# Taking the small loads' wait at the first chunk instead of the third, in a two-layer encoder kernel

## The reference

```python
def reference(x, norm_mix, norm_ffn, norm_final, ...):
    for i in range(DEPTH):
        h = rmsnorm(x, norm_mix[i])
        if i % N_MIXERS == 0:
            x = x + stick_breaking_mixer(h, sb_w_in[j], sb_w_out[j])
        else:
            x = x + mlstm_mixer(h, ml_w_in[j], ml_b_i[j], ml_b_f[j], ml_g_head[j], ml_w_out[j])
        h = rmsnorm(x, norm_ffn[i])
        x = x + hierarchical_moe(h, moe_w_group[i], moe_b_group[i], moe_w_expert[i], moe_b_expert[i],
                                 moe_w1[i], moe_w3[i], moe_w2[i])
    return rmsnorm(x, norm_final)
```

## Time and profile before

| | |
|---|---|
| median of 3 runs | 1768.82 us (1767.27 to 1771.22) |
| the profiled execution's own time | 1768.82 us |
| its span | 1767.1 us |
| TensorE busy (matmuls) | 1568.3 us, 89% |
| VectorE busy | 729.4 us, 41% |
| ScalarE busy | 423.4 us, 24% |
| GpSimd busy | 64.9 us, 4% |
| mean granted TensorE clock | 0.946 of full speed |

### The profile page before, as it was taken

One profiled execution on the slowest core, in us unless ns is written; L12 is line 12 of the kernel. 1 busy time (PEld: TensorE's weight loads), 2 busy tenths in 40 slices (PEclk: granted clock), 3 DMA queues, 4 the chain that ended last, 5 costly groups with the idle time before them and its releaser, 6 DMA issues.

```text
span 1767.1 us, 25607 instructions
## 1 busy us (share of the span) xinstructions
PE 1568.3 (89%) x9901; PEld 1074.5 (61%) x9901; DVE 729.4 (41%) x1167; ACT 423.4 (24%) x571; POOL 64.9 (4%) x90
## 2 busy tenths in 40 slices
PE   7999999999997788878799999999999887788775
PEld 7999999888543234423287988988864443243322
DVE  4454454443332222223264757657434232223223
ACT  5343443433000000000054334343320000000002
POOL 2210100100100000000011000000000000000000
PEclk9999999999998898889899999999999888998897
DMA  7645555578999999999954455566699999999996
GB/s 262 196 150 167 160 172 168 214 263 305 371 384 425 427 425 425 425 427 424 417 181 146 144 190 178 178 234 213 225 356 394 422 424 425 427 424 424 425 426 264
DMA packets 149643, 543.79 MB, mean 308 GB/s; under 512 B 8864, under 2 KB 25680, under 8 KB 116432
## 3 DMA queue, kind: packets, MB, share of 16 engines
q1 hardware_dynamic: 148448, 541.14, 78.8%
q0 software_dynamic: 1136, 1.82, 0.4%
HBM read 540.83 MB, written 2.10 MB: 307 GB/s over the span
## 4 chain that ended last, share of the span: by engine, by line
PE 58%; DMA 27%; issue 5%; SPq 5%; DVE 2%; ACT 2%; POOL 1%; POOLq 0%; DVEq 0%; ACTq 0%
PE psum_G L706 30%; DMA ring<-in_moe_w 26%; PE psum_S L706 16%; PE psum_A L706 7%; SPq L521 5%; PE psum_T L706 4%; DVE w_lo L421 1%; ACT w_hi L417 1%; ACT h L1365 0%; POOL arena L668 0%; ACT arena L1199 0%; PE psum_A L713 0%; DVE x L1710 0%; POOLq L642 0%; DVE h L1960 0%
## 5 line engine op out<-in xcount | busy, mean ns | idle before, releaser
L706 PE MATMUL psum_A<-ring,arena 128*32 128x512 f32 x2048 | 297.5, 711 | 146.3 <-DMA ring<-in_moe_w 142.5
L421 DVE TENSOR_TENSOR w_lo<-ring,w_hi 128x2048 fp32r<-128x2048 f32 x126 | 289.1, 2298 | 288.3 <-ACT w_hi L417 282.9
L417 ACT CAST w_hi<-ring 128x2048 fp32r<-128x2048 f32 x128 | 244.1, 1908 | 242.5 <-PE psum_G L706 154.3
L706 PEld LDWEIGHTS psum_A<-ring,arena 128*32 128x32 f32 x2048 | 68.5, 120 | 316.9 <-issue 315.1
L1843 DVE COPY arena_two<-psum_A 128x512 f32<-128x512 f32 x64 | 44.3, 692 | 382.6 <-PE psum_T L706 350.0
L1875 DVE TENSOR_TENSOR x<-x,psum_S 128x512 f32<-128x512 f32 x128 | 88.0, 688 | 168.7 <-PE psum_S L706 168.7
L706 PE MATMUL psum_G<-xT_hi,w_hi 128*128 128x256 f32 x512 | 148.7, 290 | 1.0 <-DVE w_lo L421 1.0
L706 PE MATMUL psum_G<-xT_hi,w_lo 128*128 128x256 f32 x512 | 144.8, 283 | 0.0
L706 PE MATMUL psum_G<-xT_lo,w_hi 128*128 128x256 f32 x512 | 144.7, 283 | 0.0
L706 PE MATMUL psum_G<-ring,arena_two 128*32 128x512 f32 x976 | 121.5, 618 | 16.1 <-DMA ring<-in_moe_w 16.0
L1381 ACT ACTIVATE arena_two<-psum_T 128x64 f32<-128x64 f32 x64 | 14.4, 224 | 488.6 <-PE psum_T L706 488.6
(11 more groups left out here) (239 smaller groups left out, 2124.0 us busy)
## 6 DMA issues: line engine op xcount, KB each, us to landing
ring<-in_moe_w SPq DMA_DIRECT2D x378, 1024.0 KB, 18.8
ring<-in_sb_w_in SPq DMA_DIRECT2D x48, 1024.0 KB, 5.0
ring<-in_ml_w_in SPq DMA_DIRECT2D x48, 1024.0 KB, 5.2
ring<-in_sb_w_out SPq DMA_DIRECT2D x16, 1024.0 KB, 4.9
ring<-in_ml_w_out SPq DMA_DIRECT2D x16, 1024.0 KB, 5.1
turned_slots<-in_moe_w SPq DMA_DIRECT2D x6, 1024.0 KB, 12.6
x<-in_x SPq DMA_DIRECT2D x2, 1024.0 KB, 6.0
out_x<-h SPq DMA_DIRECT2D x4, 512.0 KB, 2.8
```

The source lines that it names most:

```text
L417: act.copy(w_hi[:, slot_place(j), :], ring[:, slot_place(j), :]).then_inc(hi_made, 1)
L421: dve.tensor_tensor(w_lo[:, slot_place(j), :], ring[:, slot_place(j), :], w_hi[:, slot_place(j), :].bitcast(F32), ALU.subtract).then_inc(l ...
L706: return pe.matmul(dst, lhsT, rhs, start=start, stop=stop, skip_group_check=True)
```

## The change

The work that waits for the small loads is taken at the end of the first chunk of group 0 instead of at the end of the third: `split_gates` on ScalarE, `scale_router` on VectorE (in both layers), and `thresholds` and `gate_lo` on VectorE. No operation is added or removed, and no load is issued at another place.

```diff
@@ ScalarE, sb_group
                     if step == "chunk" and kind == "out" and k < XC - 1:
                         chunk_squares(0, k)
-                    if step == "chunk" and kind == "first" and k == 2:
+                    if step == "chunk" and kind == "first" and k == 0:
                         split_gates(act)
@@ VectorE, common_step (both layers)
                         take_chunk(layer, i, k)
-                    if kind == "first" and k == 2:
+                    if kind == "first" and k == 0:
                         scale_router(layer)
```

## The result

The changed kernel takes 1790.98 us (median of 4 runs, 1789.12 to 1791.99) against 1769.34 us for the kernel before on the same chip: 21.6 us slower, ratio 1.0121 with a 95% interval of 1.0104 to 1.0139. The forecast was 1790.2. The profiled execution took 1790.06 us; its span is 1788.3 us, against 1767.1.

What follows compares the result with a forecast made beforehand. TensorE was taken to bound the projection, the weight stream the experts. A hole of 21.3 us, plus 1.7 of clock, less 1.6 of old hole, gave +21.4 on 1768.8: 1790.2 us, range 1786 to 1798.

Steps and rivals of the forecast that it cites:

- The place of the hole: Group 0 of layer 0: TensorE, done with slot 6 at 58.0, waits for slot 7 until 79.3, 21.3 us.
- The pace of the small loads: GpSimd's eight `gate_w` loads: one at a time, 2.66 us for each interval once slot loads stop.
- The rival that kept the 5.5 us: Small loads keep their pace, 20th lands at 90.50 as before: +37 us, 1806; chance 0.06.
- the rival with 0.75 us: Small loads limited by issue time alone, 20th lands at 61.5: +8.1 us, 1777; chance 0.04.
- The landing: Last of the 20 small loads, awaited by ScalarE and VectorE: lands at 74.8, bounds 71.7 and 81.7.
- From the landing to TensorE: Slot 7: 2.25 us from landing to the next `w_lo`, which takes 2.29; 4.5 us in all.
- The clock: TensorE at the start of slot 7: half rate for 3.4 us after idling, costing 1.7 us, bounds 0 and 3.4.
- The hole that goes: Chunk 2 of group 0: TensorE's 1.6 us wait for GpSimd's mask vanishes, -1.6 us, bounds 0 and -1.6.
- Layer 1: `scale_router` moves behind the q/k chunk, where its 0.76 us fit VectorE's idle 1.40 us: cost nothing.
- No absorption: Experts' stage: everything shifts by the same 21 us; the rival, delay absorbed beside the weight stream, stays at 1768.8, chance 0.03.
- The sum: Whole kernel: 21.3 + 1.7 - 1.6 = +21.4 us, giving 1790.2 us.
- the three terms: TensorE's hole before slot 7 (21.3 us), the slow clock after it (1.7), the vanishing mask wait (-1.6).

Runs made afterwards that it cites:

- the doubled loads: Changed kernel with each of the eight `gate_w` loads issued a second time into a place of its own, 28 small loads counted: 1813.08 us, ratio 1.0220.
- the second run of VectorE's: Kernel before with only VectorE's `scale_router` moved to chunk 0, measured once more: 1789.47 us, ratio 1.0111.
- those with TensorE kept busy: Changed kernel with matmuls of constants on TensorE ahead of slot 7: 92 gave 1788.64 us (ratio 1.0113), 104 gave 1789.26 us (1.0132 upper bound, ratio 1.0114).
- the output-stage version: Kernel before with layer 0's four pieces of work moved to the output stage's first chunk: ratio 0.9965, then 1766.60 us, ratio 0.9982, when measured again.

## Why the prediction was right

**The place of the hole**: TensorE was done with slot 6 at 57.8 (58.0 by the rows of before) and waited for slot 7 alone. Shown by the timelines, and by the two kernels that move one wait each.

**The pace of the small loads**: 2.66 us for an interval was taken from one of seven intervals, and 2.58 was measured; the doubled loads give the same 2.58 over fifteen. The kernel with the wait at chunk 1 has the pace change when the slot loads stop. The rival that kept the 5.5 us is refuted by all of these, and the rival with 0.75 us too.

The reason given for the 2.66 was partly misread. The slot's load was not nearly through when the fourth small load was issued at 65.51: 325 of its 528 packets moved in that interval, nearly all in the first 1.5 us. In the changed kernel's quiet queues a `gate_w` load moves no packet in the first 1.4 us behind its issue (52.82 to 54.2) and all 32 in the next 0.9. So what was left of the slot's load passed before the small packets moved anyway. The load issued at 51.46 had moved none after 3.1 us. That it is held back beside a slot load is thus shown; whether its packets stood in their queue by then, or came to it late, is not.

The quiet pace has an exception that the changed kernel's trace doesn't show and the others do. Five intervals without any slot packet took 3.2 to 4.2 us, in the runs with one engine's part alone (3.4, and 4.2 in the second run of VectorE's) and in those with TensorE kept busy (3.2, 4.0, 4.1). These five are also the only ones without slot packets in which a packet of a queue named `instruction` moved. The prediction had no such term; where such intervals came, they made the landing 0.6 to 3.0 us later. Whose instructions they were, and why a small load waits for them, the traces don't show.

**The landing**: 74.8 predicted, 74.83 measured, which is luck, since three of the terms were off by more and cancelled. The first `gate_w` was issued at 52.82 and not at 51.46 (+1.4), the seven intervals were 0.5 us shorter in sum, and the last load landed in 1.6 us and not 2.4 (-0.8). The first of these is the one that was thought fixed: it lay between 51.2 and 55.5 over the runs with a wait at chunk 0 or 1, and at 58.3 in one of the output-stage version, with the `router_w` loads ahead of it moving as well. With the wait at chunk 0 and all 20 loads, the landing lay between 74.35 and 77.39. The fit of the Trainium skill (DMA: Bandwidth & Descriptors, anatomy of one DMA) gives an estimate of 2.04 us for 16 KB; measured here in quiet queues are 2.2 to 2.4, and for the few bytes of `gate_b`, where the estimate is 2.0, mostly 1.6.

**From the landing to TensorE**: 4.5 us predicted, 79.42 - 74.83 = 4.6 measured. The hole: 21.3 predicted, 21.7 measured.

**The clock**: the mechanism was right, the size a bit small. 1.7 us was taken from a hole of 3.7 us; 2.3 was measured, 4.8 us at half. The runs with ScalarE's or VectorE's part alone and with doubled loads lost 1.7 to 1.8 each (a hole of 21 us or of 45 alike), those at chunk 1 and without `gate_w` loads, with holes of 7.4 and 3.0 us, 2.6 and 2.8. The length of the hole doesn't set it; what does is open. The rule that an idle TensorE falls back to half rate (TensorE: Matmul & The Clock Gate, Part 1, of the Trainium skill) holds in every trace with a hole of 2.7 us or more; behind the old hole of 1.6 us the clock stayed at 1.00.

**The hole that goes**: 1.6 predicted, 1.8 measured, alone in the output-stage version and inside the changed kernel.

**Layer 1**: cost nothing, as predicted. VectorE's timeline in the changed kernel:

```profile
944.64 1.28 DVE L1508 TENSOR_TENSOR arena<-psum_G,arena 128x512 f32<-128x512 f32 x2
945.84 0.75 DVE L1528 TENSOR_TENSOR router_w<-router_w,scales 128x576 f32<-128x576 f32 x1
947.32 0.41 DVE L1671 TENSOR_TENSOR arena<-psum_T,arena 8x256 f32<-8x256 f32 x1 [0.74 <-PE psum_T L706]
```

Against the earlier trace rows the idle time before the gates has shrunk from 1.40 to 0.74, and the gates do not start later.

**No absorption**: the distance of 22.2 us at the output stage is 22.0 at layer 1's start, with the whole experts' stage between. The rival fell on what it was tested for.

**The sum**: +21.4 predicted, +21.6 measured. By the trace the three terms make 21.7 + 2.3 - 1.8 = 22.2, which is 0.8 above the prediction's, and the 0.8 came back later, most of it at the start of layer 1, for which the prediction had no term. In the trace with ScalarE's part alone 1.3 us came back. So the mechanism was right, and part of the closeness of the number is luck too.

## What to carry to other kernels

In a stream of hand-written order a wait holds all that stands behind it, here the split of a slot that had nothing to do with the small loads. Before moving such a wait forward, compare its due time with the landing in the trace, and work out the landing anew, since the stall itself empties the queues that made it late. And look at the wait's old place too: it was late there as well, and moving it back instead of forward took away a hole of 1.8 us.

## What the runs showed of the hardware

The 16 KB loads of `gate_w`, issued by GpSimd, came one at a time: each was issued some 0.27 us after the one before had landed, every 2.5 to 2.7 us in quiet queues, every 3.2 to 4.2 in five quiet intervals with an `instruction` packet, and every 2.6 to 6.1 us beside 1 MB loads. The four smaller loads behind them were issued back to back, at some 0.5 us each.

What a hole of TensorE costs behind its end did not grow with its length: 1.7 us of lost clock behind 2.7 us of idling and behind 45, and as much as 2.8 behind 3.0.
